# In the first attention, the slices of the next queries' projection stand in one run per unit instead of two

## The reference

```python
def window_gqa_sink(h, w_qkv, w_out, sink):
    qkv = h @ w_qkv
    q = qkv[..., :H_A * HEAD_DIM].reshape(b, s, KV_A, G_A, HEAD_DIM)
    k = ...; v = ...
    # query t attends keys s with |s - t| <= 128, bias -slope * |s - t|
    o, lse = banded_attention(q, k, v, slopes, 1, WINDOW_A, BLOCK_A)
    o = o * sigmoid(lse - sink)
    return o @ w_out
```

## Time and profile before

| what | value |
|---|---|
| median of 3 runs | 2705.15 us (2703.63 to 2705.7) |
| the profiled execution's own time | 2706.37 us |
| its span | 2705.1 us |
| PE busy | 2579.3 us (95%) |
| DVE, ACT, POOL busy | 791.5, 943.4, 794.9 us |
| mean granted clock of TensorE | 0.952 |
| the 32 units | from 51.3 us (first scores) to 181.9 us |

### The profile page before, as it was taken

How to read it: one execution, slowest core, us unless ns; L and a number is a source line. 1 busy time by engine, 2 the same in 40 slices (tenths; PEclk the granted TensorE clock), 3 DMA queues, 4 the chain that set the end, 5 groups by cost and what they waited for, 6 DMA issues and landing times. The chain is left out here.

```text
span 2705.1 us, 30203 instructions
## 1 busy us (share of the span) xinstructions
PE 2579.3 (95%) x12788; PEld 2023.4 (75%) x12788; DVE 791.5 (29%) x1283; ACT 943.4 (35%) x1424; POOL 794.9 (29%) x336
## 2 busy tenths in 40 slices
PE   8999999999999999999999999997998899899898
PEld 5777888877788778877786777876884677675676
DVE  3643222003111121121104222106205553422661
ACT  5443333224333333343324333214226332333531
POOL 3123444443333233233214656442220001231001
PEclk9999999999999999999879999998999898899899
DMA  3122222223221122222112333222120000221001
GB/s 122 40 71 70 94 94 94 94 93 109 73 76 64 61 78 71 68 66 71 55 34 99 131 129 130 94 94 101 62 68 8 1 1 27 99 86 59 1 1 63
DMA packets 53287, 192.66 MB, mean 71 GB/s; under 512 B 6688, under 2 KB 7968, under 8 KB 52256
## 3 DMA queue, kind: packets, MB, share of 16 engines
q1 hardware_dynamic: 49104, 179.47, 19.9%
q10 hardware_dynamic: 4048, 11.24, 1.2%
HBM read 188.60 MB, written 2.10 MB: 70 GB/s over the span
## 5 line engine op out<-in xcount | busy, mean ns | idle before, releaser
L210 POOL TENSOR_TENSOR w_lo<-w_raw,w_hi 128x1024 fp32r<-128x1024 f32 x332 | 794.7, 2397 | 1887.2 <-ACT w_hi L147 1887.2
L147 ACT ACTIVATE w_hi<-w_raw 128x1024 fp32r<-128x1024 f32 x332 | 350.5, 1057 | 680.4 <-DMA w_raw<-in_wstream 673.4
L153 PE MATMUL ps<-h_hi,w_hi 128*128 128x512 f32 x1360 | 552.9, 407 | 12.2 <-DVE dvS L1018 5.3
L155 PE MATMUL ps<-h_hi,w_lo 128*128 128x512 f32 x1360 | 543.1, 399 | 0.0
L154 PE MATMUL ps<-h_lo,w_hi 128*128 128x512 f32 x1360 | 543.1, 399 | 0.0
L153 PEld LDWEIGHTS ps<-h_hi,w_hi 128*128 128x128 f32 x1360 | 259.7, 191 | 80.2 <-issue 13.4
L155 PEld LDWEIGHTS ps<-h_hi,w_lo 128*128 128x128 f32 x1360 | 258.5, 190 | 61.5
L154 PEld LDWEIGHTS ps<-h_lo,w_hi 128*128 128x128 f32 x1360 | 259.5, 191 | 58.4
L511 ACT ACTIVATE da_prob<-da_prob,da_nm 128x768 f32<-128x768 f32 x64 | 59.9, 936 | 274.8 <-DVE da_nm L504 274.8
L1923 PE MATMUL ps<-l_kT,j_qc 96*128 96x256 f32 (+1 forms) x288 | 117.1, 530 | 15.4 <-ACT j_qc L1987 15.4
L153 PE MATMUL ps<-l_h_hi,w_hi 128*128 128x512 f32 (+3 forms) x352 | 126.1, 358 | 0.0
(11 more groups left out here) (276 smaller groups left out, 3910.8 us busy)
## 6 DMA issues: line engine op xcount, KB each, us to landing
w_raw<-in_wstream SPq DMA_DIRECT2D x332, 512.0 KB, 3.3
l_dft<-in_dft ACTq DMA_DIRECT2D x4, 1024.0 KB, 6.4
x<-in_x SPq DMA_DIRECT2D x4, 512.0 KB, 5.7
out<-x SPq DMA_DIRECT2D x1, 2048.0 KB, 6.3
dist<-in_dist ACTq DMA_DIRECT2D x1, 1536.0 KB, 7.1
l_wuq<-in_wuq ACTq DMA_DIRECT2D x2, 768.0 KB, 5.7
y<-in_ctx SPq DMA_DIRECT2D x1, 1024.0 KB, 8.9
l_wukv<-in_wukv ACTq DMA_DIRECT2D x2, 512.0 KB, 3.3
```

The costliest lines, as they stand in the source:

```text
L147: self.A.activation(self.w_hi[:, n % RING, :], self.w_raw[:, n % RING, :], ACT.Copy).then_inc(self.w_high, 1)
L153: T.matmul(out, wh, ah, start=start, stop=False)
L155: return T.matmul(out, wl, ah, start=False, stop=stop)
L210: G.tensor_tensor(c.w_lo[:, n % RING, :], c.w_raw[:, n % RING, :], c.w_hi[:, n % RING, :].bitcast(F32), ALU.subtract).then_inc(c.w_low, 1)
```

## The change

In `WindowAttention.tensor`, all slices of a unit stand ahead of `turn_probs`; `turn_probs` and `sum_values` follow one another directly. In unit 0 all three slices stand ahead of the scores. In units 28 to 31 `modulation` stands ahead of `turn_probs`, where it stood behind. Behind the change all lines of the file have numbers smaller by 2 (line 770 is 768).

```diff
-            half = (done + goal) // 2
             if u == 0:
-                self.slices(0, half)
+                self.slices(0, goal)
             if u < self.UNITS:
                 self.scores(u)
             if u % 4 == 1 and u > 4:
                 self.spread_out_of(u // 4 - 1)
             if u:
-                self.slices(done, half)
+                self.slices(done, goal)
+            if 28 <= u < self.UNITS:
+                self.modulation(u - 28)
             if 1 <= u <= self.UNITS:
                 self.turn_probs(u - 1)
-            self.slices(half, goal)
-            if 28 <= u < self.UNITS:
-                self.modulation(u - 28)
             if u >= 2:
                 self.sum_values(u - 2)
```

## The result

The changed kernel takes 2725.95 us (median of 6 runs, 2723.13 to 2730.42), the kernel before beside it 2705.36 us (6 runs, 2701.63 to 2708.84): 20.6 us or 0.8% slower, ratio 1.008, interval 1.0067 to 1.0093. Forecast were 2717.0 us and a range of 2709 to 2722. The direction was right, the size outside the range. The profiled execution has a span of 2728.4 us; PE's busy time grew from 2579.3 to 2593.2 us although it runs the same instructions, and the mean granted clock fell from 0.952 to 0.948.

A forecast was written before the change was run, and what follows sets the result against it. PE was taken as the bound, its waits paid in full. Terms 0 + 0.54 + 0.44 + 2.80 + 5.8 + 2.2 = 11.8 us over the median 2705.15 gave 2717.0 us, range 2709 to 2722.

The forecast's parts named there:

- Bound and switches: PE bounds the stage; in units 1 to 27 the direct switch from transposes to values adds 0 us.
- Units 0, 9, 16, 20, 24, 28: Scores of unit 1 later by 0.54 us, unit 9's values by 0.44, four waits for new tiles' queries +2.80 together.
- The port: Units 17, 21, 25: POOL's subtraction holds DVE's copy to wrden on their shared port and PE waits; +5.8 us in all.
- rival B: The copy to wrden is not held up and the rest stays: 2709 to 2711 us; 14%.
- a chunk ends, DVE evacuates it, and the scores of a new tile wait: Units 16, 20, 24, 28: evacuation behind the later copy of the probabilities delays the scores by 0.70 us each, +2.80.
- Units 28 to 33: Moved modulation makes unit 28's invert meet POOL's subtraction, so the next spread waits; +2.2 us, bounds -1.2 and +2.8.
- the last wait stays at 3.65 us: End of stage: the last invert misses POOL's start again, so the earlier units' 2.2 us stay to the end.
- The clock: No clock loss in the sum; falls considered only at new idle times, about 1.5 us each.
- rival D: The clock falls at the new idle times, about 1.5 us each; with all four 2723 us; 8%.
- no fall at 2.02 us: Profile row where a PE idle time of 2.02 us left the granted clock at 1.00, window 10 to 35.

The follow-up runs named there:

- a_all_back: Changed kernel with one slice ahead of unit 0's scores, modulation in its old place, later weight splits and evacuation ahead of the copy; 2708.09 us against 2706.98, ratio 1.0009.
- a_late_split: Changed kernel with ScalarE's weight-block split in units 16, 20, 24 and 28 one unit later; 2717.65 us against 2705.11 for the kernel before, ratio 1.0052.
- after_again: The changed kernel unaltered, run again for a second profile; 2727.65 us against 2709.33 for the kernel before, ratio 1.007.
- a_fill_last: Changed kernel with seven extra 128x512 matmuls ahead of the wait for wrden at unit 29; 2727.54 us against 2705.11 for the kernel before, ratio 1.0082.
- b_last_late: Kernel before with ScalarE's last weight-block split of the stage moved behind the exponential of the last tile's sinks; 2709.77 us against 2706.98, ratio 1.0005.
- b_mod_new: Kernel before with only the modulation moved ahead of the transposes in units 28 to 31; 2720.75 us against 2706.98, ratio 1.0042.
- b_mod_end: Kernel before with the modulation moved behind the values in units 28 to 31; 2711.87 us against 2707.12, ratio 1.0027.

## Why the prediction was wrong in size

**Bound and switches.** PE is the bound and every wait up to unit 28 was paid in full; the direct switch from transposes to values costs what two switches over a slice cost. Right, by the table and by a_all_back.

**Units 0, 9, 16, 20, 24, 28.** 0.56, 0.44 and four times 0.70 against 0.54, 0.44 and 0.70. Right.

**The port.** 1.88 us three times against 1.96, 1.92, 1.92; rival B is out, since the copy was held as the tensor_scalar was. a_late_split shows the cause by taking it away. The rule of the Trainium skill ("SBUF — State Buffer", section "Who interferes with whom") that a copy in a two-port mode contends, and whichever starts second waits for the whole instruction, is in line with this: 2.27 us against 0.43. That this copy runs in such a mode no run shows directly.

**Unit 13: a term left out, 1.23 us.** The step "a chunk ends, DVE evacuates it, and the scores of a new tile wait" was carried out for the queries alone. The chunk of keys ends in unit 12, and the spread of unit 13 waits for the same evacuation, behind the copy and the invert.

**Units 28 to 33: 8.6 to 9.5 us where 2.2 were forecast.** The collision was there, with 1.96 us of idle PE where some 2.0 were forecast (0.77 in after_again, where PE was already slow). With the clock kept up to the last spread (a_fill_last) the part cost 3.2 us. So 1.0 us of the miss has nothing to do with the low clock ahead of that spread, and 0.4 of it lies behind the spread, where that profile's clock was low as well. The other 5.4 to 6.3 are the clock, by this one profile. The forecast that the last wait stays at 3.65 us failed too: it was 0.83 and 0.15 us, since PE came to it late.

**The clock: the step that failed.** The sum put the clock at nothing, and moving the modulation cost in it only the collision, 2.2 us. The text took the clock as a matter of the new idle times alone (rival D, 8%, 1.5 us for each fall). Two things happened. Idle times of 1.8 us were followed by one fall in four of the six profiles that have them (at 143.3, 141.9, 140.7 and 161.0 us, 1.5 to 1.6 us each), by none in the 11 profiles without them; my row for "no fall at 2.02 us" was one row. And the modulation, moved for no cost of its own, brought the larger part: the clock was low for 13.6 to 27.3 us in units 28 to 33 in all six profiles in which the modulation stands elsewhere than between transposes and values and no fillers are there, in one of the four with it in its old place, and in none of the seven with fillers. In the first profile 11.8 forecast, 1.2 for unit 13, 1.5 for the fall at 143, 5.4 for the low clock and 1.0 at the end are 20.9, against 20.8 in the stage; in after_again, without the fall and with 6.3 for the low clock, 20.3 against 20.2. The timed runs say the same in the large: at an equal mean clock the changed kernel costs some 13 us, which is the forecast and the spread of unit 13, and the rest goes with the clock.

**Open.** Why the clock falls so much more often when the 16 narrow matmuls stand elsewhere within a unit is not settled: the units hold the same instructions in either order, and one profile with the old order (b_last_late) has the low clock too. That it is the low clock and not the order that costs the time is shown by the fillers in the profiles, and by b_mod_new and b_mod_end at an equal mean clock. How often the clock is low in units 28 to 33 of the executions without a trace is not known. Nor is it known why the medians differ from what the stages say by up to 6.8 us, beyond that most of it goes with the mean clock.

## What to carry to other kernels

When a step moves on one engine, follow every instruction that is queued behind it on the engines that consume it, and ask of each whether it now meets an instruction of GpSimd that reads SBUF; an unchanged engine can be held for 2 us by a shift of 0.7. For every such late result list all who wait for it, not only the one in view. In a stretch where PE runs matmuls of a few columns, a new order of the same instructions is not free until the granted clock of that stretch has been looked at in more than one profile. And when timed runs scatter, compare them at an equal mean clock as well as by their medians.

## What the runs showed of the hardware that was not expected

PE was busy for 20.00 of 20 us, by the profile, and its granted clock was 0.52 there. In the 20.5 us at the lower level it started 42 matmuls of 2 or 4 moving columns and 68 of 128. With four matmuls of 512 columns more in each unit the clock was 1.00 in the same units up to the wait for the last spread, in all four profiles that have them, and in b_mod_fill and a_fill_units the stage was shorter for it (4.3 us late and not 9.5, and 14.9 where after_again has 20.2), although nobody needs that work. Not every order of the same instructions lost the clock: it was 1.00 from 156 to 176 us in the kernel before. A DVE reciprocal from SBUF to SBUF ran its usual 0.20 us under GpSimd's subtraction, while the copy behind it was held.
